# A 32-expert router rewritten around the eight-largest instruction, a gather from reordered tokens, and dummy matrix products at four places

## What is computed

```
g_logit = xt @ w_group + b_group                      # 4 groups
g_sel = argmax(g_logit)
e_logit = (xt @ w_expert + b_expert).reshape(t, 4, 8)[chosen group]
top_p, top_i = top_k(softmax(e_logit), 2)             # 2 experts of 8
gate = g_w * top_p / sum(top_p)
y = silu(xb @ w1[e]) * (xb @ w3[e]) @ w2[e]           # for the tokens of expert e
out = sum over the token's two experts of gate * y
```

## Time and profile before

| | us |
|---|---|
| median of 3 runs (1150.2 to 1153.31) | 1150.59 |
| the profiled execution, its time | 1149.9 |
| its span, first to last instruction | 1148.1 |
| PE busy / DVE busy / ACT busy in the span | 949.9 / 528.4 / 359.9 |
| mean granted TensorE clock, share of full | 0.938 |

### The profile page before, as it was taken

The page is one execution under the profiler, slowest core; times in us unless marked ns, Lnnn a source line. Parts: engine busy times, 40 slices in busy tenths (PEclk is TensorE's granted clock), DMA queues, the critical chain, the costliest instruction groups (busy, mean ns, idle before and its releaser), DMA issues.

```text
span 1148.1 us, 23491 instructions
## 1 busy us (share of the span) xinstructions
PE 949.9 (83%) x10355; PEld 839.9 (73%) x10355; DVE 528.4 (46%) x859; ACT 359.9 (31%) x541; POOL 46.3 (4%) x43
## 2 busy tenths in 40 slices
PE   5999999889999997999999877757675767576654
PEld 5999998889999996899988866645454545454542
DVE  4545766756655656778876641212121212121212
ACT  4444555454333335343656421010100010001011
POOL 0100001300000000000110200000000000000000
PEclk9999999899999999999999979998889698889897
DMA  9754423646555553445434977999999999999993
GB/s 333 228 184 138 152 69 111 230 135 214 183 180 186 183 176 119 154 144 181 148 132 158 346 318 288 404 428 427 428 429 429 428 429 429 428 429 429 429 427 140
DMA packets 109521, 310.02 MB, mean 270 GB/s; under 512 B 5685, under 2 KB 92409, under 8 KB 96665
## 3 DMA queue, kind: packets, MB, share of 16 engines
q1 hardware_dynamic: 107712, 304.66, 69.6%
q0 software_dynamic: 1008, 4.20, 1.0%
q10 hardware_dynamic: 744, 0.35, 0.1%
HBM read 308.14 MB, written 1.05 MB: 269 GB/s over the span
## 4 chain that ended last, share of the span: by engine, by line
PE 53%; issue 41%; DVE 3%; ACT 1%; POOL 1%; DMA 0%; ACTq 0%; POOLq 0%; DVEq 0%
PE ps L682 16%; PE ps L683 16%; PE ps L684 16%; PE ps L937 1%; DVE w_lo L1334 1%; PE ps L848 1%; PE ps L836 0%; PE ps L780 0%; DMA rows<-in_g_mix 0%; PE ps L826 0%; PE ps L815 0%; PE ps L814 0%; DVE h L1424 0%; POOL stat L628 0%; ACT junk L1194 0%
## 5 line engine op out<-in xcount | busy, mean ns | idle before, releaser
L682 PE MATMUL ps<-x_hi,w_hi 128*128 128x256 f32 x928 | 266.6, 287 | 0.0
L683 PE MATMUL ps<-x_lo,w_hi 128*128 128x256 f32 x928 | 262.7, 283 | 0.0
L684 PE MATMUL ps<-x_hi,w_lo 128*128 128x256 f32 x928 | 262.7, 283 | 0.0
L1334 DVE TENSOR_TENSOR w_lo<-arena,w_hi 128x2048 fp32r<-128x2048 f32 (+3 forms) x83 | 166.3, 2006 | 53.5 <-ACT w_hi L1076 53.0
L1011 PE MATMUL ps<-arena,xg 128*32 128x128 f32 x3968 | 133.4, 295 | 59.4 <-DMA arena<-in_w 52.3
L682 PEld LDWEIGHTS ps<-x_hi,w_hi 128*128 128x128 f32 x928 | 177.2, 191 | 5.4 <-issue 4.3
L683 PEld LDWEIGHTS ps<-x_lo,w_hi 128*128 128x128 f32 x928 | 177.3, 191 | 1.6 <-issue 1.0
L684 PEld LDWEIGHTS ps<-x_hi,w_lo 128*128 128x128 f32 x928 | 177.2, 191 | 0.2
L1011 PEld LDWEIGHTS ps<-arena,xg 128*32 128x32 f32 x3968 | 120.1, 119 | 76.0 <-DMA arena<-in_w 63.6
L1076 ACT ACTIVATE w_hi<-arena 128x2048 fp32r<-128x2048 f32 (+3 forms) x83 | 138.4, 1670 | 37.7 <-PE ps L684 27.9
L1021 PE MATMUL ps<-arena,hid_T 128*32 128x256 f32 x992 | 72.0, 439 | 55.4 <-DMA arena<-in_w 35.7
(11 more groups left out here) (272 smaller groups left out, 1291.9 us busy)
## 6 DMA issues: line engine op xcount, KB each, us to landing
arena<-in_w SPq DMA_DIRECT2D x90, 2048.0 KB, 23.3
arena<-in_w_in SPq DMA_DIRECT2D x43, 1024.0 KB, 5.3
arena<-in_w_ffn_in SPq DMA_DIRECT2D x22, 1024.0 KB, 5.1
arena<-in_w_ffn_out SPq DMA_DIRECT2D x11, 1024.0 KB, 4.9
arena<-in_w_out SPq DMA_DIRECT2D x8, 1024.0 KB, 6.1
arena<-in_w SPq DMA_DIRECT2D x6, 1024.0 KB, 9.3
third_w<-in_w SPq DMA_DIRECT2D x3, 2048.0 KB, 12.8
arena<-in_w_mem_kv SPq DMA_DIRECT2D x2, 1024.0 KB, 5.9
```

Of the source, the lines that this page charges most:

```text
L682: mm(dst, l_hi, r_hi, start=start, stop=False)
L683: mm(dst, l_hi, r_lo, start=False, stop=False)
L684: return mm(dst, l_lo, r_hi, start=False, stop=stop)
L1334: v.tensor_tensor(w_lo[:, u % 3, 0:n], ring[:, u % 3, 0:n], w_hi[:, u % 3, 0:n].bitcast(F32), ALU.subtract).then_inc(lo_ready, 1)
```

## The change

The diff has five parts.

1. **Router.** The masked logits are made by one addition of 0 or -1e30, the eight-largest instruction (`v.max`) finds the best of 32 for each half of the tokens, and `match_replace` marks the two largest; one comparison gives `chosen`. Three small instructions (two fills and `slot_no`) now stand ahead of the sum of squares. The exponentials' input follows after `route_sel`, and the gates (`gate_weights`) follow after `one_hot`.
2. **Counting.** Three matrix products ahead of `rank` become two, and the two for the count of passes go to a bank and a semaphore of their own.
3. **Gather.** ACT writes the scaled tokens to a new place `n3g` in the order in which the gather reads them, so that the gather's stationary operand is contiguous and ACT's read has the 32-byte step instead. `n3g` lies over the part of the constant table that is not used any more at that point; for that `before` moves ahead in the table.
4. **Dummy products.** `keep_warm(n, bank)` issues n float32 products of `ones` with `ones` (128 x 128 with 128 columns), whose result nobody reads: 14 before the first tokens are turned, 20 after `row(0)`, 16 at each residual boundary.
5. **In the router,** 16 such products between the last `route_logits` and the wait for `route_sel`.

```diff
+        def keep_warm(n, bank):
+
+            for _ in range(n):
+                mm(ps[:, bank, 0:P], ones[:, :], ones[:, :], start=True, stop=True)
...
+                pe.wait_ge(ones_ready, 1)
+                keep_warm(14, 0)
...
                 row(0)
+                keep_warm(20, 0)
...
             elif step == "residual":
+                keep_warm(16, 6 if arg[0] == 0 else 0)
...
         route_logits(3)
+        for _ in range(16):
+            mm(ps[:, 2, 0:P], ones[:, :], ident, start=True, stop=True)
         pe.wait_ge(route_sel, 1)
 
-        before = const("before")
-        mm(ps[:, 1, 0:EXPERTS], before, chosen[:, 0, :], start=True, stop=True)
-        mm(ps[:, 1, EXPERTS:2 * EXPERTS], before, chosen[:, 1, :], start=True, stop=False)
-        mm(ps[:, 1, EXPERTS:2 * EXPERTS], ones[:, :], chosen[:, 0, :], start=False, stop=True)
-        mm(ps[:, 1, 64:64 + EXPERTS], ones[:, :], chosen[:, 0, :], start=True, stop=False)
-        mm(ps[:, 1, 64:64 + EXPERTS], ones[:, :], chosen[:, 1, :], start=False, stop=True).then_inc(rank_done, 1)
+        mm(ps[:, 1, 0:2 * EXPERTS], const("before"), chosen[:, :, :].rearrange("p b e -> p (b e)"), start=True,
+           stop=False)
+        mm(ps[:, 1, EXPERTS:2 * EXPERTS], ones[:, :], chosen[:, 0, :], start=False, stop=True).then_inc(rank_done, 1)
+        mm(ps[:, 5, 0:EXPERTS], ones[:, :], chosen[:, 0, :], start=True, stop=False)
+        mm(ps[:, 5, 0:EXPERTS], ones[:, :], chosen[:, 1, :], start=False, stop=True).then_inc(count_done, 1)
...
-                    last = mm(ps[:, 2 + c // 4, P * (c % 4):P * (c % 4) + P], n3[:, tb, c:D:KC],
+                    last = mm(ps[:, 2 + c // 4, P * (c % 4):P * (c % 4) + P], n3g[:, tb, c, :],
                               one_hot[:, tb, :], start=tb == 0, stop=tb == 1)
...
         act.wait_ge(root_done, moe_event + 1)
-        act.wait_ge(route_T, 4)
         for tb in range(TB):
-            fn(n3[:, tb, :], n3[:, tb, :], ACT.Copy, scale=stat[:, moe_event, 6 + tb:7 + tb]).then_inc(n3_ready, 1)
+            fn(n3g[:, tb, :, :], n3[:, tb, :].rearrange("t (p c) -> t c p", c=KC), ACT.Copy,
+               scale=stat[:, moe_event, 6 + tb:7 + tb]).then_inc(n3_ready, 1)
...
+        v.memset(masked_e[:, :, EXPERTS:], PAD)
+        v.memset(top2[:, :, :], PAD)
+        link(v.tensor_scalar(slot_no[:, :], const("slot"), 1.0, None, ALU.add))
...
+        link(v.tensor_reduce(gmax, lg, AX.X, ALU.max))
+        tt(pick_g[:, :, :], lg, wide(gmax, GROUPS), ALU.is_equal)
+        tt(pick_g[:, :, :], pick_g[:, :, :], const("revg").unsqueeze(1).to_broadcast([P, TB, GROUPS]), ALU.mult)
+        link(v.tensor_reduce(place, pick_g[:, :, :], AX.X, ALU.max))
+        tt(pick_g[:, :, :], pick_g[:, :, :], wide(place, GROUPS), ALU.is_equal)
+        link(v.tensor_scalar(pick_g[:, :, :], pick_g[:, :, :], 1.0, -NEG, ALU.subtract, ALU.mult))
+
+        own = pick_g[:, :, :].unsqueeze(3).to_broadcast([P, TB, GROUPS, PER_GROUP])
+        real = masked_e[:, :, 0:EXPERTS]
+        tt(real.rearrange("p b (g e) -> p b g e", g=GROUPS), le.rearrange("p b (g e) -> p b g e", g=GROUPS), own,
+           ALU.add)
+        for tb in range(TB):
+            link(v.max(best8[:, tb, :], masked_e[:, tb, 0:EXPERTS]))
+        link(v.tensor_copy(top2[:, :, 0:2], best8[:, :, 0:2]))
+        for tb in range(TB):
+            link(v.match_replace(left_e[:, tb, :], top2[:, tb, :], masked_e[:, tb, :], TAKEN))
+        v.tensor_scalar(chosen[:, :, :], left_e[:, :, 0:EXPERTS], TAKEN / 2 + PAD / 2, None, ALU.is_lt)\
+            .then_inc(route_sel, 1)
...
-        first_of(chosen[:, :, :], masked_e[:, :, :], best, const("rev"), EXPERTS, place)
...
-        first_of(pick_one[:, :, :], masked_e[:, :, :], second, const("rev"), EXPERTS, place)
...
-        link(v.tensor_scalar(slot_no[:, :], const("slot"), 1.0, None, ALU.add))
...
+            if not looped:
+                gate_weights()
```

More of the change, by code:

```diff
@@ L45 @@
 TAKEN = -3e38
+PAD = -2.5e38
 TOPK = T // 4
@@ L57 @@
 _at = 0
-for _name, _n in (("ident", P), ("later", P), ("before", P), ("rotate", P), ("keep", CAUSAL), ("hide", CAUSAL),
+for _name, _n in (("ident", P), ("before", P), ("later", P), ("rotate", P), ("keep", CAUSAL), ("hide", CAUSAL),
                   ("cos", 2 * T), ("sin", 2 * T), ("slot", SLOTS), ("rev", EXPERTS), ("revg", GROUPS), ("steps", 8)):
@@ L291, in layers_kernel @@
     gain_rows = [put(f"gain_row{i}", [P, D], F32) for i in range(2)]
+    tab_at = at
     tab = put("tab", [P, TABLE_W], F32)
@@ L364, in layers_kernel @@
     n3 = nc.alloc_sbuf_tensor_at("n3", [P, TB, D], F32, offset=o_at)
+    assert TABLE["sin"][1] - TABLE["later"][0] == TB * D
+    n3g = nc.alloc_sbuf_tensor_at("n3g", [P, TB, KC, P], F32, offset=tab_at + 4 * TABLE["later"][0])
     n3T = nc.alloc_sbuf_tensor_at("n3T", [P, KC, T], F32, offset=o_at + 8192)
@@ L1562, in ffn @@
             split(S2 + 3 * (NF - 1) + 2)
-        v.memset(ones[:, :], 1.0).then_inc(dve_chain, 1)
-        chain[0] += 1
+        v.memset(ones[:, :], 1.0).then_inc(ones_ready, 1)
+        dve.wait_ge(ones_ready, 1)
         used = 0
@@ L1722, in _ @@
-        gmax, place, gsum, best, second, total, share = (r_s[:, i, :] for i in range(7))
-        lg, le = logits[:, :, 0:GROUPS], logits[:, :, GROUPS:36]
-        biggest(gmax, lg, GROUPS)
-        tt(exp_in[:, :, 0:GROUPS], lg, wide(gmax, GROUPS), ALU.subtract)
-        first_of(pick_g[:, :, :], lg, gmax, const("revg"), GROUPS, place)
-        own = pick_g[:, :, :].unsqueeze(3).to_broadcast([P, TB, GROUPS, PER_GROUP])
-        dst, hidden = (t[:, :, :].rearrange("p b (g e) -> p b g e", g=GROUPS) for t in (masked_e, pick))
@@ L1748, in _ @@
-        link(v.tensor_reduce(total, exp_out[:, :, GROUPS:36], AX.X, ALU.add))
-        link(v.reciprocal(total, total))
-        tt(gate_e[:, :, :], exp_out[:, :, GROUPS:36], wide(total, EXPERTS), ALU.mult)
-        tt(gate_e[:, :, :], gate_e[:, :, :], chosen[:, :, :], ALU.mult)
-        link(v.tensor_reduce(share, gate_e[:, :, :], AX.X, ALU.add))
-        link(v.reciprocal(share, share))
-        tt(share, share, gsum, ALU.mult)
-        tt(gate_e[:, :, :], gate_e[:, :, :], wide(share, EXPERTS), ALU.mult)
+        gmax, place, gsum, _, _, total, share = (r_s[:, i, :] for i in range(7))
@@ L1759, in _, with gate_weights @@
                                     ALU.mult))
+        def gate_weights():
+            dve.wait_ge(route_exp, 1)
+            link(v.tensor_reduce(gsum, exp_out[:, :, 0:GROUPS], AX.X, ALU.add))
+            link(v.reciprocal(gsum, gsum))
+            link(v.tensor_reduce(total, exp_out[:, :, GROUPS:36], AX.X, ALU.add))
+            link(v.reciprocal(total, total))
+            tt(gate_e[:, :, :], exp_out[:, :, GROUPS:36], wide(total, EXPERTS), ALU.mult)
+            tt(gate_e[:, :, :], gate_e[:, :, :], chosen[:, :, :], ALU.mult)
+            link(v.tensor_reduce(share, gate_e[:, :, :], AX.X, ALU.add))
+            link(v.reciprocal(share, share))
+            tt(share, share, gsum, ALU.mult)
+            tt(gate_e[:, :, :], gate_e[:, :, :], wide(share, EXPERTS), ALU.mult)
         def count_passes():
-            link(v.tensor_reduce(r_s[:, 8, 0:1], ps[:, 1, 64:64 + EXPERTS], AX.X, ALU.max))
+            dve.wait_ge(count_done, 1)
+            link(v.tensor_reduce(r_s[:, 8, 0:1], ps[:, 5, 0:EXPERTS], AX.X, ALU.max))
             link(v.tensor_scalar(exp_in[:, 0, 0:8], const("steps"), r_s[:, 8, 0:1], None, ALU.is_lt))
```

33 lines of the change are left out of this document (7 added, 26 removed).

## The result

The changed kernel takes 1137.12 us in the median of 4 runs (1136.32 to 1138.37), the kernel before, timed beside it, 1151.55 of 4 (1150.2 to 1153.31): ratio 0.9874, 95% interval 0.9857 to 0.989. The profiled execution spans 1134.6 us against 1148.1. The direction was right, the size was not.

The account below looks back on a forecast made before the run. Experts are bound by their weights (DMA at 426 GB/s); the router delays the stream's restart. Router 6.8, start 1.8 and two boundaries 0.5 each sum to 9.6 us: 1150.6 - 9.6 = 1141.0 us, range 1138.0 to 1146.5.

Parts of the forecast that it names:

- What restarts the stream: Ahead of the expert stream: an earlier L1011 brings the weight loads and the end forward one for one, below 9.4 us.
- The router: Logits to first expert products: new routing, dummies and contiguous gather start L1011 at 686.7, a gain of 6.8 us.
- `chosen`: Router: 15 instructions after the logits' two take 3.5 us instead of 5.1, so it is complete at 679.8.
- the dummies, not the routing, release the counting: Router: the 16 dummies end at 680.5, 0.7 us after `chosen` is ready, and so release the counting.
- ACT's strided copy: Ahead of the gather: both copies take 2.19 to about 3.9 us, end by 679.7 and cost nothing.
- The gates: DVE during the gather: gate work ends at 685.6, just before the gather's 685.8, so the gates cost nothing.
- The first boundary: First residual boundary: dummies bring full clock to the transposes and gain 0.5 us, bounds 0 and 0.58.
- The start: Start to first unit: dummies bring full clock, gaining 0.85 before DVE's copy and 0.95 in the unit, together 1.8 us.
- The second boundary: Second residual boundary: dummies gain 0.5 us as at the first, bounds 0 and 0.58.
- "the DMA engines are busy all the time at 426 GB/s": Expert loop, 715 to 1100 us: bound by weights, so a faster gather there gains nothing.
- "all at full clock": Rival: `chosen` releases counting 0.7 earlier and the last w2 takes near 2 us, not 3.52: 1138.6 us, chance 0.10.
- The rule on transposes: Start and boundaries, rival: transposes don't keep the clock up, so start gains 0.2, boundaries nothing: 1143.6 us, chance 0.08.

Follow-up runs that it names:

- e5: Changed kernel, but the seven gathers inside the loop over quads read tokens with the old 32-byte step; quad 0 stays contiguous: 1137.61 us, 0.9886.
- e3: Kernel before with the reordered tokens and contiguous gather alone, old routing, no dummies: 1149.14 us, 0.9982.
- e10: Changed kernel with the router's 16 dummies alone, none at the start or the residual boundaries: 1141.67 us, 0.9929.
- e6: Changed kernel with 8 instead of 16 dummy products in the router: 1140.78 us, 0.9915.
- e12: As e6, but with 8 more dummies ahead of the start's first transposes (22 instead of 14): 1139.07 us, 0.9895.
- e8: Changed kernel plus 12 dummies ahead of each layer's first output unit and 22 instead of 16 at the second residual boundary: 1138.32 us, 0.9893.
- e2: Kernel before with all the changed kernel's dummy products and nothing else of it: 1146.05 us, 0.9949.
- e1: Changed kernel without any dummy product, routing and gather as changed: 1145.39 us, 0.9953.
- e11: Kernel before with all of e8's dummies but the router's, no other change: 1145.5 us, 0.9955.

## Why the prediction was right and wrong

*Right, by its own steps.* What restarts the stream: L1011's start moved SP's load one for one, 2.01 us in both. The router by 7.1 us against 6.8. Within it: the logits came 0.1 us later behind L876, not 0.3; `chosen` was complete 3.50 us behind them (4.05 forecast); the dummies, not the routing, release the counting, 4.50 behind the logits (4.75 forecast); gather 3.81 us (3.8). ACT's strided copy took 4.23 us for both halves instead of 2.19, above the bound of 3.9, and cost nothing. The gates ended at 680.4 and were hidden. A faster gather in the loop gains nothing (e5). The first boundary gained 0.45 (0.5), and does so every time: R1 to R2 takes 198.0 in all nine profiles with dummies there, 198.4 to 200.5 in the five without.

*Right by luck in part.* The start gained 1.5 (1.8), with L778 to DVE's copy in 0.82 us, not 0.49; but with no dummies at all it took 30.0 and 30.4 us in e3 and e10, against 29.9. The second boundary gained 0.45 (0.5), but four of six profiles with the same dummies took 230.4 to 230.8 us there, 2 us more than before.

*Wrong: the sum ended there.* "Sum. 6.8 + 1.8 + 0.5 + 0.5 = 9.6" took each place as if nothing changed at any other. Three items stood at nothing, and they are 3.9 us, the whole difference between 9.6 and 13.5.
- The stream, 1.4 us. That "the DMA engines are busy all the time at 426 GB/s" was read from a window that begins at 715, behind two of the pauses. Ahead of it PE lost 2.7 us to them, and DMA ran at 397 GB/s from 705 to 715 and at 365 from 735 to 745. They depend on where PE's instructions lie (e6 against e12), so an edit of PE's program can move them. That a pause is a late load of instructions is argued from the packets, not shown. Nor does a pause set the loss: e8 has pauses of 1.52 and 1.95 us and a stream of 431.3, e2 none above 0.37 and one of 432.4. How much of the 1.4 us is theirs stays open.
- The tail, 1.6 us. The text had the size, in "all at full clock", but called it luck with 0.10. Of fourteen profiles eight ended in 18.0 to 18.1 us, five in 19.5 to 20.8 and one in 22.0. So it is luck, but in these profiles better than even, and the 19.6 of one profile was not the value to start from.
- M to R1, 0.9 us: the clock's low stretch at the first output unit, where no dummies stand. Chance can account for it. With no dummy ahead of it the clock was low there for 6.8 us (before, e1), 3.4 (e3) or not at all (e10, M to R1 208.9).

*What is chance in the result.* The start, M to R1, the second boundary and the tail vary in this way. Over nine runs of the changed kernel in two sittings the median is 1137.83, so the gain is nearer 13 than 14.4 us, and the second sitting's 1138.45 lies inside the forecast's range. The bigger error in reasoning was to price the dummies place by place against one profile. The low stretches differ from one execution to the next: against the profiles without dummies the start's blocks give 0.1 to 1.5 us and the first boundary's 0.4 to 2.5. Together the blocks outside the router are worth 3.2 to 4.6 us (e10), and with e8's additions 5.0 (e11).

*The rule on transposes.* In e3, and in e10 too, the clock came back at the start while PE did nothing but transposes (four records in 0.71 us right behind them, 1.22 before), so the forecast was right to weigh against it. The Trainium skill, TensorE: Matmul & The Clock Gate, Part 4, says that transposes do not count as activity; these traces do not agree.

ACT's read with the 32-byte step took 1.9 times its contiguous time, the weight loads 337 against 192 ns:

```profile
L1002 PEld LDWEIGHTS ps<-one_hot,n3g x256: 186/192/338, 678.3 to 1072.1; 128*128 128x128 f32 x128
```

The Trainium skill, SBUF — State Buffer, section "Door 1: The DMA port swizzle", says that each crossing to a new 16-byte line costs; the trace agrees, for ACT too. For the weight loads it agrees at full clock alone: at half clock contiguous ones take 333 ns too (e6, 679 to 682 us), about as long as those with the step at either level (312 to 342).
